# First attention of a three-layer network: bias rows written once, norms and transposes moved into the q and gate units, groups of heads overlapped

## What is computed

```python
q = _rmsnorm(q.reshape(bsz, L, N_Q_HEADS, HEAD_DIM), q_norm_g)
k = _rmsnorm(k.reshape(bsz, L, N_KV_HEADS, HEAD_DIM), k_norm_g)
logits = einsum('bnqkgd,bnskd->bnkgqs', qb, kb) * (HEAD_DIM ** -0.5)
logits = where(valid, logits + bias, -inf)      # bias depends on the distance query - key alone
m = maximum(max(logits), sink);  p = exp(logits - m)
w = p / (sum(p) + exp(sink - m))
out = einsum('bnkgqs,bnskd->bnqkgd', w, vb)
```

## Time and profile before

| | us |
|---|---|
| median of 3 runs | 3406.75 (3405.16 to 3407.32) |
| the profiled execution | 3405.32 |
| its span, first to last instruction | 3403.4 |
| of it the units from the middle of `u` to the end of `ws1` | 338.9 (us 73.67 to 412.58) |

### The profile page before, as it was taken

The page is one execution under the profiler, slowest core; times in us unless marked ns, Lnnn a source line. Parts: engine busy times, 40 slices in busy tenths (PEclk is TensorE's granted clock), DMA queues, the critical chain, the costliest instruction groups (busy, mean ns, idle before and its releaser), DMA issues. The chain is left out here.

```text
span 3403.4 us, 38821 instructions
## 1 busy us (share of the span) xinstructions
PE 3266.6 (96%) x15938; PEld 2693.5 (79%) x15938; DVE 1865.5 (55%) x1978; ACT 1472.1 (43%) x1757; POOL 81.3 (2%) x76
## 2 busy tenths in 40 slices
PE   7797899999999999999999999999999999999998
PEld 5576688888888878878888888878787788888886
DVE  6355554555555554656555555565545655555555
ACT  5324354444444444445444444444444544444443
POOL 1021000000000000000000000001000000000000
PEclk9798899999999999999999999999999999999999
DMA  5324255555555645555555555555454555555554
GB/s 178 106 93 127 90 186 191 186 191 192 186 196 187 195 158 186 191 180 193 190 186 191 192 186 188 191 169 176 158 172 149 175 185 191 191 186 188 193 188 149
DMA packets 187550, 596.31 MB, mean 175 GB/s; under 512 B 12491, under 2 KB 19308, under 8 KB 186860
## 3 DMA queue, kind: packets, MB, share of 16 engines
q1 hardware_dynamic: 187372, 593.82, 53.0%
HBM read 588.54 MB, written 5.23 MB: 174 GB/s over the span
## 5 line engine op out<-in xcount | busy, mean ns | idle before, releaser
L1109 DVE TENSOR_TENSOR LO<-RAW,HI 128x1024 fp32r<-128x1024 f32 (+1 forms) x1104 | 1345.9, 1221 | 1172.3 <-ACT HI L580 1169.9
L580 ACT ACTIVATE HI<-RAW 128x1024 fp32r<-128x1024 f32 (+1 forms) x1104 | 1159.1, 1052 | 1414.1 <-PE PS L1960 1331.6
L1960 PE MATMUL PS<-HI,KPA 128*128 128x512 f32 x5312 | 1485.2, 396 | 20.7 <-ACT ACC L634 9.7
L1960 PEld LDWEIGHTS PS<-HI,KPA 128*128 128x128 f32 x5312 | 1002.0, 191 | 234.7 <-issue 17.3
L1960 PE MATMUL PS<-HI,KPB 128*128 128x512 f32 x3392 | 936.1, 393 | 3.5 <-DVE ACC L1668 3.4
L1960 PE MATMUL PS<-LO,KPA 128*128 128x512 f32 x2656 | 834.3, 395 | 10.0 <-DVE LO L1109 10.0
L1960 PEld LDWEIGHTS PS<-HI,KPB 128*128 128x128 f32 x3392 | 631.8, 188 | 132.7 <-issue 5.0
L1960 PEld LDWEIGHTS PS<-LO,KPA 128*128 128x128 f32 x2656 | 505.1, 190 | 120.9 <-DVE LO L1109 12.6
L1960 PE MATMUL PS<-LO,KPB 128*128 128x512 f32 x1696 | 525.0, 391 | 0.0
L1960 PEld LDWEIGHTS PS<-LO,KPB 128*128 128x128 f32 x1696 | 318.8, 188 | 68.0 <-issue 0.5
L607 ACT ACTIVATE KPB<-PS 128x512 fp32r<-128x512 f32 x98 | 58.5, 598 | 181.4 <-PE PS L2018 181.4
(11 more groups left out here) (259 smaller groups left out, 1059.1 us busy)
## 6 DMA issues: line engine op xcount, KB each, us to landing
RAW<-in_w_up SPq DMA_DIRECT2D x128, 1024.0 KB, 4.9
RAW<-in_w_down SPq DMA_DIRECT2D x128, 1024.0 KB, 5.4
RAW<-in_w_qkv SPq DMA_DIRECT2D x48, 1024.0 KB, 5.0
RAW<-in_w_ff_gate SPq DMA_DIRECT2D x88, 512.0 KB, 3.7
RAW<-in_w_ff_up SPq DMA_DIRECT2D x88, 512.0 KB, 4.6
RAW<-in_w_ff_down SPq DMA_DIRECT2D x44, 1024.0 KB, 5.4
RAW<-in_w_in_ab SPq DMA_DIRECT2D x40, 1024.0 KB, 4.9
RAW<-in_w_in SPq DMA_DIRECT2D x16, 1024.0 KB, 16.2
```

The lines of the kernel that those rows point to most:

```text
L580: e.activation(HI[:, s % NSPLIT, 0:w], RAW[:, d % NRAW, j, 0:w], ACT.Copy).then_inc(S("hi_made"), 1)
L1109: e.tensor_tensor(LO[:, h, 0:w], RAW[:, d % NRAW, j, 0:w], HI[:, h, 0:w].bitcast(F32), ALU.subtract).then_inc(S("lo_made"), 1)
L1960: ins = e.matmul(PS[:, b + j, 0:cw], l, r[:, h, 512 * j:512 * j + cw], start=(i == 0 and part == 0), stop=(last and part == 2))
```

## The change

The bias rows are written once, 16 rows of 383, turned round (the one-hot table is reversed), behind the fourth load of `u`. `bias(g)` reads overlapping windows of a row, one element further for each partition, and DVE reads the tile backwards.

k's squares, sums and root move into `q` (`k_norm`); q's norm, KD and all the transposes move into `glu` (`q_norm`, `attn_prep`, started by `late(attn1(), 4)` after four steps), now through banks 4 and 5, so after the last use by the state-space lanes. Between gate and `ws0` there are the last two sets of transposes (they follow the gate's last step) and group 0's scores.

Groups overlap: a second logits tile LG1 and a second set of small tiles let group n+1's scores and logits stand ahead of group n's transposes and products. `mids` gives the generator one `next` between the two token tiles of a step, `sides` one after it. Buffers move (KD onto an earlier tile; qT and kT 32 KB up).

```diff
-                    src = bass.AP(scratch.tensor, (4 * g + h) * 128 * 384 + 127 + off, [[383, 128], [1, width]])
+                for c0, width in ((256, 128), (0, 256)):
+                    src = bass.AP(scratch.tensor, (4 * g + h) * 384, [[1, 128], [1, width]])
...
-            if dma_of("u", 6) <= d < dma_of("u", 6) + 8:
-                h = 2 * (d - dma_of("u", 6))
+            if d == dma_of("u", 6):
                 q.wait_ge(S("bias_rows_made"), 1)
-                e.dma_start(scratch[h:h + 2, :, 0:383], bcast(WV[h:h + 2, :], 1, 128)).then_inc(S("bias_written"), 16)
+                e.dma_start(scratch[:, 0:383], WV[0:16, :]).then_inc(S("bias_written"), 16)
...
-def in_units(n, feeder, sides, ends, ahead, step, have=0):
+def in_units(n, feeder, sides, ends, ahead, step, have=0, mids=()):
+    def between():
+        for g in mids:
+            next(g, None)
...
-        step(i)
+        step(i, between if i < n - 1 else None)
...
+            q.wait_ge(S(f"bias{n}"), 128)
+            q.wait_ge(S(P + "scores"), 4 * n + h + 1)
+            e.scalar_tensor_tensor(out=lg[:, h, :], in0=PS[:, 4 + h % 2, 0:384], scalar=0.125, in1=backwards(BT[n % 2][:, h, :]),
...
+        def attn1():
+            yield from attn_prep()
+            for h in range(4):
+                scores1(0, h)
+                if h % 2:
+                    yield
...
+            for n in range(4):
+                if n < 3:
+                    for h in range(4):
+                        scores1(n + 1, h)
+                        if h % 2:
+                            yield
+                for h0 in (0, 2):
+                    for h, bank in ((h0, 4 + h0 // 2), (h0 + 1, 5 - h0 // 2)):
+                        q.wait_ge(S(P + "weights"), 4 * n + h + 1)
+                        q.wait_ge(S(P + "logits"), min(4 * n + 8, 16))
...
-        unit("glu", None, [S0, S1], ahead=1)
-        att = attn1()
-        for _ in range(6):
+        att = late(attn1(), 4)
+        unit("glu", None, [S0, S1, att], ahead=1)
+        for _ in range(2):
             next(att)
-        unit("ws0", None, [s_sums(), att, att])
-        unit("ws1", None, [att, att])
+        unit("ws0", None, [s_sums(), att], mids=[att])
+        unit("ws1", None, [att], mids=[att])
         drain(att)
```

More of the change, by code:

```diff
@@ L43, in bcast, with backwards @@
     return bass.AP(ap.tensor, ap.offset, dims)
+def backwards(ap):
+    (ps, pn), (s, n) = [list(d) for d in ap.ap]
+    return bass.AP(ap.tensor, ap.offset + s * (n - 1), [[ps, pn], [-s, n]])
 class Unit:
@@ L581, in hi, with unit, step @@
                 split[0] += 1
-        def unit(name, feeder=None, sides=(), ends=(), evac=None, hold=False, ahead=5, have=0):
+        def unit(name, feeder=None, sides=(), ends=(), evac=None, hold=False, ahead=5, have=0, mids=()):
             u = U[name]
-            def step(i):
+            def step(i, between):
                 if not (hold and i == u.nk - 1):
                     hi(u.first + i + LA)
-            in_units(u.nk, feeder, sides, ends, ahead, step, have)
+                if between is not None:
+                    between()
+            in_units(u.nk, feeder, sides, ends, ahead, step, have, mids)
             if evac is not None:
@@ L1339, in ssm, with k_norm @@
                 yield
[L1341 to L1344, removed]
+        def k_norm():
+            for _ in range(9):
                 yield
[L1346 to L1359, removed]
             for t in range(2):
@@ L1366, in attn_prep, with q_norm @@
             yield
+        def q_norm():
             yield
+            for t in range(2):
+                q.wait_ge(S("q_squared"), t + 1)
+                e.tensor_reduce(sqs[:, 16 * t:16 * t + 16], heads(SQ[:, :], 16), X, ALU.add).then_inc(S("q_summed"), 1)
+                yield
+            q.wait_ge(S("q_summed"), 2)
+            mean("q", sqs, 64, EPS)
             q.wait_ge(S("root_made"), ROOT["k"])
-            for p in range(2):
-                q.wait_ge(S(f"ssm{p}_y"), 4)
             for t in range(2):
@@ L1524, in vector @@
             gate_times(n)
-        for _ in range(6):
+        for _ in range(2):
             next(att)
         sS = s_stats()
-        unit("ws0", sf, [sS, att, att], [sS], add_x(0, "S"), have=1)
+        unit("ws0", sf, [sS, att], [sS], add_x(0, "S"), have=1, mids=[att])
         added("ws0")
-        unit("ws1", None, [att, att], (), add_x(1, "S"))
+        unit("ws1", None, [att], (), add_x(1, "S"), mids=[att])
         added("ws1")
@@ L1918, in gpsimd, with q_root @@
         unit("q", [S0, S1])
-        unit("glu", [S0, S1])
-        root("q")
         root("k")
+        def q_root():
+            for _ in range(4):
+                yield
+            root("q")
+            yield
+        unit("glu", [S0, S1, q_root()])
         for name in ("S", "A", "ln2", "pre0", "vn", "mix0", "mpre0", "mlp0", "pre1"):
@@ L1965, in matmuls @@
                     ins.then_inc(S("tile0_done"), 1)
+                if t == 0 and between is not None:
+                    between()
         def gate(u, i, h, kt, ks):
@@ new lines, in scores1 @@
+        def scores1(n, h):
+            P = "at0_"
+            q.wait_ge(S("qk_turned_out"), 6)
+            if h >= 2:
+                q.wait_ge(S(P + "logits"), 4 * n + h - 1)
+            elif n:
+                q.wait_ge(S(P + "logits"), 4 * n)
+            if n >= 2:
+                q.wait_ge(S(P + "written"), 4 * n - 4)
+            rows = slice(64 * (h % 2), 64 * (h % 2) + 64)
+            qq, kk = qT[rows, 2 * n + h // 2, :], kT[rows, n, :]
+            e.matmul(PS[:, 4 + h % 2, 0:128], qq[:, 0:128], kk[:, 0:128], start=True, stop=True)
+            e.matmul(PS[:, 4 + h % 2, 128:384], qq[:, 128:256], kk, start=True, stop=True).then_inc(S(P + "scores"), 1)
```

248 lines of the change are left out of this document (163 added, 85 removed).

## The result

The changed kernel takes **3331.07 us** (median of 4 runs, 3326.39 to 3331.98) against 3406.9 of the kernel before (4 runs, 3405.16 to 3407.32): a ratio of 0.9776, 95% interval 0.9759 to 0.9793. The forecast was 3332 us, with a range of 3313 to 3357.

The account below looks back on a forecast made before the run. PE bounds most of the kernel, with idling in `u` and `q` from loads held up by slow bias-row writes. Terms -51 + 3.5 - 6 - 20 = -73.5 against 3405.32 gave 3331.8, said as 3332 us; range 3313 to 3357.

Parts of the forecast that it names:

- rival C: Loads in `u` and `q` slow for their own sake, not by the writes: 3383 us in total; chance 0.03.
- Part 1: Second half of `u`, first half of `q`: bias rows written once, 69.6 for 120.4 us, -51 (-55 to -40).
- 4.5 us of other waits: PE waits unrelated to loads in `u` and `q`: 2.7 by the preceding stretch's rate, 2 for bank handover.
- The write itself: The single 24.5 KB bias-row write under loads in `u`: at most 1.1 us, taken as nothing.
- Part 2: Gate: norms and transposes moved into it lengthen it by 3.5 us (+2 to +7).
- Part 3: Stretch between gate and `ws0`: 9 us for 15.07, -6 (-3 to -8).
- Part 4: `ws0` and `ws1` with overlapping groups: 84 us for 104.3, -20 (-34 to -8).
- DVE's chain: `ws0`, `ws1`: logits, maximum, small operations and LO, 4.8 us before DVE's copy; 2 us wait for each of three groups.
- A: DVE becomes the bound of `ws0` and `ws1`: saving there 8 instead of 20 us, total 3344; chance 0.20.
- B: Preparation in `u` is a second bound under the late loads: saving there 40 us, total 3343; chance 0.10.
- D: Overlapping bias reads before `ws0` crawl, deciding below some 25 GB/s: +24 us, total 3430; chance 0.03.
- the waits for PT: `ws0` and `ws1`: sign expected in the trace, PE waits of 2 us for PT by DVE.

Follow-up runs that it names:

- part 1 alone: Kernel before with only the single bias-row write, overlapping reads and backward mask; attention and its preparation as before: 3348.25 us, ratio 0.9828.
- a_again: The changed kernel unaltered, run once more on another chip: median 3327.36 us; its profiled execution took 3332.56 us.
- both undone: Changed kernel with groups of heads one after another and both attention pieces at each step's end, without half-step places: 3339.32 us.
- a_gate_first: Changed kernel with the last two q transpose sets in banks 6 and 7 and ACT opening the gate before copying them out: 3326.16 us.

## Why the prediction was right

**What bounds the kernel: right.** The late loads were the bound of `u`, by the writes: part 1 alone gives 59 of 76 us, and rival C is out.

**Part 1: right in kind, 6 us too small**, beyond its bound of -55. Two terms were mis-sized. I counted sixteen steps of PE between two marks that hold fifteen (60 matmuls with LO at 4 a step in the trace after), 2.7 us too many for its own work: 62.5 measured for 65.1. And I added 4.5 us of other waits; PE idles 1.1 there. The stretch before does idle 3.1 of 29 us still, so that rate was real, but it doesn't carry over to the next stretch. PE's products with LO there (count; busy us and mean ns; idle time before them):

```profile
L2054 PE MATMUL PS<-LO,KPA 128*128 128x512 f32 x60 | 18.8, 395 | 0.2 <-DVE LO L1155 0.2
```

**The write itself:** I costed it at nothing, and nothing shows: issued at us 45.14, landed in 5.1 us. The Trainium skill's rule on how many engines share a transfer (DMA: Bandwidth & Descriptors, "Why a DMA increments its semaphore by 16 and not by 1") fits the busy shares in the traces, 0.12 and 0.89 of 16 engines. The speed doesn't follow that number: sixteen rows went 4 times as fast as two (99 against 25 GB/s), not eight.

**Part 2: right, +3.6 for +3.5**, as seen from the kernel before and in the faster execution; the gate of the other, 47.85 us, gives +5.4. The Trainium skill's rule that DVE and GpSimd exclude each other (SBUF — State Buffer, "Who interferes with whom") speaks of this place. Timeline of POOL and DVE of the changed kernel:

```profile
216.98 0.93 POOL L1948 TENSOR_TENSOR LANE<-LANE,LANE 128x256 f32<-128x256 f32 x1 [5.76 <-DVE LANE L1384]
...
218.92 5.45 POOL L1925 TENSOR_TENSOR ST<-ST,NEG 128x32 f32<-128x32 f32 x1
...
216.90 2.55 DVE L1411 TENSOR_TENSOR KD<-kv_sb,ST 128x256 f32<-128x256 f32 x4
219.38 0.68 DVE L1597 TENSOR_TENSOR KPA<-ACC,KPA 128x512 fp32r<-128x512 f32 x1
219.98 1.21 DVE L1155 TENSOR_TENSOR LO<-RAW,HI 128x1024 fp32r<-128x1024 f32 x1
```

Root, chunk and LO lie over one another, and the two DVE instructions, with two SBUF inputs each, take their usual time: beside the root the trace disagrees, as it did in the earlier trace rows. Beside POOL's work for the scan it agrees in kind: the four products for KD take 2.55 us, where they took 1.43 with POOL idle. I had sized them at 1.43 here too.

**Part 3: right in kind, 1 us too much.** 10.16 us for 9. The chain was the one I had written down, ACT's copies, table load, sigmoids, products, logits, and I had named the loss by ACT's order; what I didn't see is that the order can be had the other way round for 7.4 us.

**Part 4: right as a sum, by terms that were not.** 84.57 us for 84, but the 10 us of waits in it were to be DVE's chain, and PE waits 1.5 us for a copy by DVE, not 2 in each of three groups. PE idles 6.6 (84.57 less 77.98): two shorter waits for logits (one of 0.7 behind group 3's bias tile, sized at 2), 1.8 for squares that `s_sums` needs, 2.1 for a HI behind ACT's exponentials. Busy PE at a mean clock of 0.92 gives 77.98 x 0.92 = 72 us of own work for 74, and the low clock the other 6. A stretch of 13 us around `s_sums` runs at 0.61:

```profile
277.00:290.00 13.00, 11.32 (x52) 10.64 (x53) 3.49 (x7) 3.43 (x11) 0.00 (x0) 0.61 0.00 0
```

I had no term for the clock in the new stage, and too many waits; the two errors met, by luck. In the other profiled execution the same stages take 88.09 us at a clock of 0.89. I had also put the whole of part 4 down to the groups' order and places. By the runs these are 8 to 12 us, and the rest comes with the emptied gap ahead of `ws0`.

**The total: near by luck too.** The parts as measured in the first trace give -78.9, not -73.5, and that execution is the fastest of its four. The median came to 3331.07, beside the forecast 3332, because part 1 gave 6 us more than I had counted, and the other three executions of that series are 4 to 6 us longer than the profiled one. In `a_again`, 6.2 us longer, 5.4 of that lie from the gate to the end of `ws1`, at a lower clock. The second series has its median at 3327.36.

**The rivals.** A, DVE as the bound: not so, DVE is busy 49.59 of 84.57 and hardly waited for. B, a second bound in `u`: not so, PE idles 1.1 us. D, crawling reads: the mechanism is there, reads of the same memory land in 4.1 us for 2.4, but 128 KB in 4.1 us are 32 GB/s for each of several reads that run at a time, above the 25 from which it would have decided, and only DVE waits for one of them, 2.3 us.

**What would show it.** Loads in 5.3 us, no ACT wait for RAW, `q` ending at us 193.7 (said: near 200), `ws0` and `ws1` at 84.57 and clock 0.92: as said. The gap of 10.16 and the waits for PT: off, as told.

## What to carry to other kernels

A write from few rows of SBUF ahead of loads on one queue costs by how long it lasts, not by its bytes; spread it over rows, or write once and read with overlap. An engine that carries the chain between two units should have nothing in front of that chain that can go behind it: here, opening the gate before copying and taking the next unit's start out from behind the logits was worth about as much as overlapping whole groups. When two edits cover the same waits, undo them apart and together before saying what each is worth. And before a stage's length in one trace is read to a few microseconds, look at the same stage in a second trace of the same kernel.

## What was unexpected of the hardware

- 128 partitions reading windows of the same 1.5 KB, one element apart, land 128 KB in 4.1 us; from 128 copies, 2.4 us.
- One DMA that writes 128 copies of each of sixteen rows moves 99 GB/s with the 16 engines 0.89 busy, where loads reach 399.
- With two narrow writes issued on ACT's queue, each further issue held ACT for 12 to 15 us (six of eight); such an issue is not free of the engine's time.
- The clock behind a gap is not set by the gap alone: the first 26 us of `ws0` ran at 0.74 after 16.57 us at 0.58 (part 1 alone), at 0.90 after 10.16 at 0.77 (both undone), at 0.95 and 0.96 after 10.16 at 0.79 and 10.32 at 0.77 (the changed kernel), and at 0.90 after only 7.42 at 0.89 (`a_gate_first`).
- Two executions of one kernel, with the same waits to within half a microsecond, took 84.57 and 88.09 us for the same two stages, at a mean clock of 0.92 and 0.89.
